# Pair transfers issued by ScalarE instead of GpSimd, and the value read moved ahead of the softmax division on VectorE

## The chip, the cores and the metric

The kernel runs on one core of one Trainium2 chip. The metric is the device time of one launch in microseconds, the median of three runs. Everything is float32: each weight and each activation is split into a high part and a low part, and a product is three matmuls on TensorE.

## The reference

Two transformer blocks for 512 tokens of width 1024. The change lies in the second layer of the first block, the dilated attention:

```python
u = h @ w_in
q, k, v, gate = split(u)                     # 3 groups x 8 heads x 64 each; gate 8 x 64
q = partial_rope(rms_norm(q, q_norm), cos, sin)
k = partial_rope(rms_norm(k, k_norm), cos, sin)
for g, (window, dilation) in enumerate(((128, 1), (512, 4), (2048, 16))):
    o, lse = dilated_band_attention(q[g], k[g], v[g], dilation, window // dilation)
o = softmax-weighted sum of the three o      # weights: softmax over the three lse
x = x + (o * silu(gate)) @ w_out
```

The rotation mixes the first 16 channels of each head: channel d needs channel d + 8, or d - 8. Channels lie on the partitions here, so another partition's values are needed.

## The kernel before

Five engines run programs of their own that meet in semaphores. Each engine takes its own instructions in order. The launch is a list of 15 stages; the change is in stage 4 alone.

**Work of stage 4.** The input projection has 40 weight tiles. They are taken as four chunks (`c` = 0 to 3) of ten steps (`j` = 0 to 9), one tile for each step. A tile is 24 matmuls (8 blocks, three products each) into PSUM bank 0 or 7 in turn. Tiles 0, 1, 3, 4, 5, 6 of a chunk are queries and keys of two heads (`QK_TILES`, `n` counts them from 0 to 23), tiles 2, 7, 8 are values (`V_TILES`), tile 9 is the gate. Chunk c makes the projections of heads 2c and 2c + 1, and beside them the attention of chunk a = c - 1 is computed, in eight units (head half times residue of the position modulo 4). A fifth round (c = 4) has only attention.

**TensorE in step j of chunks 1 to 3**, in this order: the tile (L1599); if j is odd and at least 3, the products of two units with the values (`two_values`, L1823), which need ScalarE's copies of the turned probabilities; the turning of unit j - 1's probabilities, six transposes (`turn_probs`, L1837), which wait for `p_done`; the scores of the next unit (L1794, L1806); in steps 3, 8 and 9 the turning of a value tile (L1887), which for the value tile of step 7 waits until VectorE has done the variance of all six query and key tiles (`var_done`); in steps 1, 2, 4, 5, 6, 7 the sum of squares of the tile before (L1650).

**VectorE in step j**: the variance of tile j - 2 (`head_var`, L995, only if that is a query or key tile; then the tile is finished in this step); maxima of unit j - 1 (L1265 to L1270) and of unit j (L1272); the low part of a coming weight tile (`prep`, L973), which waits for ScalarE's high part; the softmax division of unit j - 1 (reciprocal L1284, multiplication L1285, which gives `p_done`) after ScalarE's exponential; in steps 2, 7, 8 and 9 the read of the value or gate tile j out of PSUM (L1298, L1293), which waits until TensorE has finished tile j; then three instructions of Newton's step (L988 to L990) from ScalarE's guess of 1/sqrt; and the rotation of tile j - 2, four instructions (L1305 to L1308), which gives `n_done`. The rotation reads `at_pair`, where the 16 channels of each head lie with their partners' values. `at_pair` has two buffers, used in turn.

**ScalarE in step j**: the high part of a coming weight tile (`prep`, L457); the copy of the turned probabilities of unit j - 2 (L457, two instructions, `at_PT`); the exponential of unit j - 1 (L717); the guess for 1/sqrt from the variance (`guess_var`, L495 and L496); for a query or key tile the copy out of PSUM into `at_raw` (L457) and the square (L476).

**GpSimd** does nothing in this stage but issue the transfers that fill `at_pair`: four for each query or key tile, 96 in all, each 8 partitions of 512 elements from `at_raw`. For tile n it waits for ScalarE's copy, and for `n_done` of tile n - 2, so that the buffer is free. Tile n - 2 in this counting is: for the tile of step 3, that of step 0 (rotated in step 2); step 4, that of step 1 (rotated in step 3); step 5, that of step 3 (rotated in step 5); step 6, that of step 4 (rotated in step 6); for steps 0 and 1, the ones of the chunk before that were rotated in steps 7 and 8.

Weights are fetched by SyncE, four tiles ahead at most. ScalarE issues some other transfers between its instructions (L638, L667, L690, L691).

Of the kernel before, what the change touches and what calls it, by code (L numbers as in the profile page):

```python
# [66 lines left out]
READ0 = [4 + sum(READS[:n]) for n in range(15)]  # L67
LAST = 14
BARRIERS = ()
PAIR_CLEARED = 3  # L70
PI = 3.1415925
ROUND = 1.5 * 2.0 ** 23
TURN = (6.28125, 0.0019350051879882812, 3.019916e-07)
# [77 lines left out]
def build(nc, weights, x_in, ple_in, pos_in, params_in, consts_in, masks_in, out, spill):  # L151
    ctx = ExitStack()
    with ctx:
# [241 lines left out]
        def slot_bank(j):  # L395
            return 7 * (j % 2)
# [32 lines left out]

        @block.gpsimd  # L430
        def _(pool):
            pool.wait_ge(dve_out, PAIR_CLEARED)
            for c in range(4):
                for i, j in enumerate(QK_TILES):
                    n = len(QK_TILES) * c + i
                    raw = at_raw[:, 6 * (c % 2) + i, :]
                    pool.wait_ge(read_out, READ0[4] + SLOTS * c + j + 1)
                    if n >= 2:
                        pool.wait_ge(n_done, KC + n - 1)
                    for h in range(2):  # L440
                        for to, of in ((0, 8), (8, 0)):
                            pool.dma_start(at_pair[h * HEAD + to:h * HEAD + to + 8, n % 2, :],
                                           raw[h * HEAD + of:h * HEAD + of + 8, :]).then_inc(pair_loaded[n % 2], 16)


        @block.scalar
        def _(act):
# [246 lines left out]
            for c in range(5):  # L694
                a = c - 1
                for j in range(SLOTS):
# [34 lines left out]
                    if c < 4:  # L731
                        k.up(tile_done)
                        k.up(read_out)
                        if j == 9:
                            act.wait_ge(read_out, k.at(read_out))
                            act.activation(at_SG[:, c % 2, :], at_SG[:, c % 2, :], ACT.Silu).then_inc(gated, 1)
                            k.up(gated)
                            logs()
                        elif j in V_TILES:
                            pass  # L740
                        else:
                            act.wait_ge(tile_done, k.at(tile_done))
                            raw = at_raw[:, 6 * (c % 2) + QK_TILES.index(j), :]
                            copy(raw, ps[:, slot_bank(j), :]).then_inc(read_out, 1)
                            act.wait_ge(read_out, k.at(read_out))
                            square(raw)
            split(at_Yh[:, 3, :], 0)
            attention_over(k, unit=(m_done, e_done, t_done, pt_done, o_done), chunk=(n_done,))
            stage_end(act, "act", k, 4)
# [209 lines left out]
        def _(dve):  # L959
# [3 lines left out]
            def link(instr):  # L963

                instr.then_inc(dve_chain, 1)
                dve.wait_ge(dve_chain, k.up(dve_chain))
# [286 lines left out]
            for c in range(5):  # L1253
                a = c - 1
                for j in range(SLOTS):
# [20 lines left out]
                    if c < 4:  # L1276
                        prep()
                        if c == 0 and j == 0:
                            newton(4, 1.0 / D, rx)
                            link(dve.tensor_scalar(ex[:, :], var[:, :], EPS, None, ALU.mult))  # L1280
                    if a >= 0 and 0 <= j - 1 < UNITS:
                        st, probs = at_st[:, u % 4, :], unit_home(a, u)
                        dve.wait_ge(e_done, UNITS * a + u + 1)
                        link(dve.reciprocal(st[:, 3:4], st[:, 2:3]))  # L1284
                        dve.tensor_scalar(probs, probs, st[:, 3:4], None, ALU.mult).then_inc(p_done, 1)  # L1285
                    if c < 4:
                        k.up(tile_done)
                        k.up(read_out)
                        if j == 9 or j in V_TILES:
                            dve.wait_ge(tile_done, k.at(tile_done))  # L1290
                        if j == 9:
                            dve.wait_ge(v_turned, GROUPS * c + 2)
                            dve.tensor_tensor(at_SG[:, c % 2, :], ps[:, slot_bank(j), :], rx[:, :], ALU.mult).then_inc(read_out, 1)  # L1293
                        elif j in V_TILES:
                            g = V_TILES.index(j)
                            if g == 2 or g == 0 and c:
                                dve.wait_ge(v_turned, GROUPS * c + (g == 2))
                            dve.tensor_tensor(value_rows(c, g), ps[:, slot_bank(j), :], rx[:, :], ALU.mult).then_inc(read_out, 1)  # L1298
                    if c < 4 and j - 1 in SUM_SLOT:
                        head_newton()  # L1300
                        n = SUM_SLOT[j - 1]
                        raw, pair = at_raw[:, 6 * (c % 2) + n, :], at_pair[:, n % 2, :]
                        even, odd = ((at_C[:, :], at_S[:, :]), (at_T[:, 0, :], at_T[:, 1, :]))[n % 2]
                        dve.wait_ge(pair_loaded[n % 2], 64 * (3 * c + n // 2 + 1))
                        dve.tensor_tensor(pair, pair, odd, ALU.mult)  # L1305
                        link(dve.tensor_tensor(raw, raw, even, ALU.mult))
                        link(dve.tensor_tensor(raw, raw, pair, ALU.add))
                        dve.tensor_tensor(raw, raw, rs[:, :], ALU.mult).then_inc(n_done, 1)  # L1308
                        dve.wait_ge(n_done, k.up(n_done))
# [996 lines left out]
```

## Time and profile before

| what | value |
|---|---|
| median of three runs | 1955.55 us (1954.84 to 1955.66) |
| time of the profiled execution | 1955.55 us |
| span of its trace | 1953.7 us |
| TensorE busy | 1894.4 us, 97% |
| VectorE, ScalarE, GpSimd busy | 64%, 44%, 3% |
| `at_pair<-at_raw` transfers | 96, 16 KB each, 1.8 us from issue to landing |
| chunk 0, chunks 1 to 3, last round of stage 4 | about 341 to 400, 400 to 654, 654 to 689 us of the span |

The trace is of one execution. Lines such as L1285 are lines of the kernel before. A row of the timeline has the start, the duration, the engine, the line, the operation, what it writes and reads, how many instructions the row merges and, in brackets, how long the engine had been idle before and on whom it waited. An instruction may begin before the recorded end of the one in front of it, since the engines are pipelined.

### The profile page before, as it was taken

The numbers are of one execution on the slowest core, as the hardware profiler recorded it, in microseconds if no ns is written. First come the engines' busy times: TensorE is split into PE (matmuls) and PEld (weight loads), VectorE is DVE, ScalarE is ACT, GpSimd is POOL, SyncE is SP. The second block draws the span as 40 slices with busy tenths as digits, with TensorE's granted clock in tenths as the row PEclk, the third lists the DMA queues.
The fourth block names the chain that finished last, engine by engine and source line by source line (L and its number), as shares of the span: only waits on it lengthen the run. The fifth ranks groups of instructions, "written<-read, shape, count | busy, mean of one in ns | idle before, by whom it ended". The sixth has DMA issues, their size and how long they took to land.

```text
span 1953.7 us, 23354 instructions
## 1 busy us (share of the span) xinstructions
PE 1894.4 (97%) x8436; PEld 1475.2 (76%) x8436; DVE 1250.8 (64%) x1960; ACT 855.2 (44%) x1207; POOL 49.5 (3%) x100
## 2 busy tenths in 40 slices
PE   6999899999999899999999999999999999999999
PEld 4888587777777677888888866666766788888887
DVE  5999888878778668444433375697766654444322
ACT  5443555445445445434332254554354444343321
POOL 0000000211111000000000000000000000000000
PEclk9999999999999899999999999999999999999999
DMA  4333143322222033332333322111221323322333
GB/s 177 97 97 97 59 145 101 110 73 70 67 70 63 30 108 98 97 104 93 100 105 114 128 65 65 54 55 54 76 65 44 112 95 98 106 95 98 97 104 101
DMA packets 51346, 175.32 MB, mean 90 GB/s; under 512 B 7616, under 2 KB 7872, under 8 KB 50624
## 3 DMA queue, kind: packets, MB, share of 16 engines
q1 hardware_dynamic: 44640, 160.19, 25.8%
q10 hardware_dynamic: 3552, 12.44, 1.7%
q0 software_dynamic: 3072, 1.58, 0.4%
q8 instruction: 53, 0.87, 0.2%
q14 instruction: 29, 0.24, 0.0%
HBM read 166.32 MB, written 6.29 MB: 88 GB/s over the span
## 4 chain that ended last, share of the span: by engine, by line
PE 71%; DVE 21%; ACT 5%; issue 3%; DMA 0%; ACTq 0%; DVEq 0%
PE ps L1599 60%; DVE cv_acc L1152 6%; DVE w_lo L973 3%; PE ps L1650 2%; PE ps L1615 1%; PE ps L1794 1%; PE ps L1837 1%; ACT w_hi L457 1%; PE ps L1806 1%; PE ps L1823 1%; DVE ds_acc L1356 1%; PE ps L1992 1%; DVE X L1025 1%; PE ps L2043 1%; DVE ds_mx L1355 1%
## 5 line engine op out<-in xcount | busy, mean ns | idle before, releaser
L973 DVE TENSOR_TENSOR w_lo<-w_raw,w_hi 128x1024 fp32r<-128x1024 f32 x299 | 365.8, 1225 | 339.8 <-ACT w_hi L457 333.7
L1599 PE MATMUL ps<-H_hi,w_hi 128*128 128x512 f32 x1272 | 508.5, 400 | 1.2 <-DVE H_lo L1019 1.2
L1599 PE MATMUL ps<-H_hi,w_lo 128*128 128x512 f32 x1272 | 495.6, 390 | 0.0
L1599 PE MATMUL ps<-H_lo,w_hi 128*128 128x512 f32 x1272 | 495.1, 389 | 0.0
L457 ACT ACTIVATE w_hi<-w_raw 128x1024 fp32r<-128x1024 f32 x299 | 313.0, 1049 | 169.8 <-PE ps L1599 169.1
L1599 PEld LDWEIGHTS ps<-H_hi,w_hi 128*128 128x128 f32 x1272 | 238.8, 188 | 59.5 <-issue 9.3
L1599 PEld LDWEIGHTS ps<-H_lo,w_hi 128*128 128x128 f32 x1272 | 238.9, 188 | 55.3 <-issue 6.7
L1599 PEld LDWEIGHTS ps<-H_hi,w_lo 128*128 128x128 f32 x1272 | 238.7, 188 | 50.8
L1599 PE MATMUL ps<-mid_hi,w_lo 128*128 128x512 f32 x352 | 138.7, 394 | 0.0
L1599 PE MATMUL ps<-mid_hi,w_hi 128*128 128x512 f32 x352 | 138.7, 394 | 0.0
L1599 PE MATMUL ps<-mid_lo,w_hi 128*128 128x512 f32 x352 | 138.7, 394 | 0.0
L1599 PE MATMUL ps<-N_hi,w_hi 128*128 128x512 f32 x280 | 118.4, 423 | 0.7 <-ACT ds_P L835 0.7
L1152 DVE SCALAR_TENSOR_TENSOR cv_acc<-cv_a,par,cv_acc 128x509 f32<-128x509 f32 (+21 forms) x176 | 116.0, 729 | 1.6 <-ACT cv_acc L608 1.6
L457 ACT ACTIVATE mid_hi<-tmp 128x512 f32 x44 | 27.8, 632 | 193.3 <-DVE tmp L1110 193.3
L1599 PE MATMUL ps<-N_hi,w_lo 128*128 128x512 f32 x280 | 112.3, 401 | 0.0
L1599 PE MATMUL ps<-N_lo,w_hi 128*128 128x512 f32 x280 | 112.1, 400 | 0.0
L1599 PEld LDWEIGHTS ps<-mid_hi,w_hi 128*128 128x128 f32 x352 | 65.8, 187 | 16.5
L1599 PEld LDWEIGHTS ps<-mid_hi,w_lo 128*128 128x128 f32 x352 | 65.8, 187 | 16.2
L1599 PEld LDWEIGHTS ps<-mid_lo,w_hi 128*128 128x128 f32 x352 | 65.8, 187 | 16.2
L1106 DVE TENSOR_TENSOR tmp<-ps,rx 128x512 f32<-128x512 f32 x44 | 30.4, 691 | 66.2 <-PE ps L1599 66.2
L1599 PEld LDWEIGHTS ps<-N_hi,w_hi 128*128 128x128 f32 x280 | 53.9, 192 | 22.7 <-issue 9.0
L1599 PEld LDWEIGHTS ps<-N_lo,w_hi 128*128 128x128 f32 x280 | 53.7, 192 | 13.7 <-issue 2.2
(342 smaller groups left out, 2713.0 us busy)
## 6 DMA issues: line engine op xcount, KB each, us to landing
w_raw<-weights SPq DMA_DIRECT2D x299, 512.0 KB, 3.5
X<-x ACTq DMA_DIRECT2D x4, 512.0 KB, 11.4
pl_P<-spill ACTq DMA_DIRECT2D x1, 2048.0 KB, 7.7
spill<-X ACTq DMA_DIRECT2D x8, 256.0 KB, 2.0
X<-spill ACTq DMA_DIRECT2D x2, 1024.0 KB, 5.0
out<-X SPq DMA_DIRECT2D x8, 256.0 KB, 4.6
at_pair<-at_raw POOLq DMA_DIRECT2D x96, 16.0 KB, 1.8
pl_raw<-ple SPq DMA_DIRECT2D x2, 512.0 KB, 12.8
```

What stands on the lines that cost most here:

```text
L457: return act.activation(out_ap, in_ap, ACT.Copy)
L973: dve.tensor_tensor(w_lo[:, s, :], w_raw[:, s, :], w_hi[:, s, :].bitcast(F32), ALU.subtract)\
L1025: dve.scalar_tensor_tensor(X[:, m:m + n, :], src, scale, X[:, m:m + n, :], ALU.mult, ALU.add)\
L1106: dve.tensor_tensor(tmp[:, j, :], ps[:, bank_of(k.n["prep"] - AHEAD - 1), :], rx[:, :], ALU.mult).then_inc(read_out, 1)
L1152: instr = dve.scalar_tensor_tensor(acc, a[:, 0:S - t], w, acc, ALU.mult, ALU.add)
L1355: link(dve.max(ds_mx[:, :], acc))
L1356: link(dve.match_replace(acc, ds_mx[:, :], acc, TAKEN))
L1599: mm = pe.matmul(ps[:, bank, :], w, x, start=first and n == 0 and q == 0, stop=last and n == len(blocks) - 1 and q == 2)
L1615: mm = pe.matmul(ps[:, banks[which], :], w, x[:, b, :], start=b == 0 and q == 0, stop=b == KC - 1 and q == 2, skip_group_check=True)
L1650: pe.matmul(ps[:, bank, :], ones if lhsT is None else lhsT, sq[:, (k.n[sq_done] - 1) % 2, :], start=c == 0, stop=c == n - 1).then_inc(sq_u ...
L1794: mm = pe.matmul(ps[:, near_bank(a, near), :], at_raw[rows, q, r:S:4], at_raw[rows, q + 1, :], start=True, stop=True)
L1806: mm = pe.matmul(ps[:, far_bank(a, far), (g - 1) * P:g * P], at_raw[rows, q + 2 * g, r:S:4], at_raw[rows, q + 2 * g + 1, r:S:4], start=Tru ...
```

## The change

GpSimd's program no longer issues anything. ScalarE issues the four transfers of a query or key tile, right after the square of that tile in its own program, with the same waits in front: the setup of VectorE for the first tile, and `n_done` of tile n - 2 for the others. On VectorE the read of the value tile or the gate tile, with its waits, now stands before the softmax division of unit j - 1 and not behind it.

```diff
         @block.gpsimd
         def _(pool):
-            pool.wait_ge(dve_out, PAIR_CLEARED)
-            for c in range(4):
-                for i, j in enumerate(QK_TILES):
-                    n = len(QK_TILES) * c + i
-                    raw = at_raw[:, 6 * (c % 2) + i, :]
-                    pool.wait_ge(read_out, READ0[4] + SLOTS * c + j + 1)
-                    if n >= 2:
-                        pool.wait_ge(n_done, KC + n - 1)
-                    for h in range(2):
-                        for to, of in ((0, 8), (8, 0)):
-                            pool.dma_start(at_pair[h * HEAD + to:h * HEAD + to + 8, n % 2, :],
-                                           raw[h * HEAD + of:h * HEAD + of + 8, :]).then_inc(pair_loaded[n % 2], 16)
+            k = Counts()
+            for stage in BARRIERS:
+                stage_end(pool, "pool", k, stage)
...
                             act.wait_ge(read_out, k.at(read_out))
+                            n = len(QK_TILES) * c + QK_TILES.index(j)
                             square(raw)
+                            if n == 0:
+                                act.wait_ge(dve_out, k.at(dve_out))
+                            if n >= 2:
+                                act.wait_ge(n_done, normed + n - 1)
+                            for h in range(2):
+                                for to, of in ((0, 8), (8, 0)):
+                                    act.dma_start(at_pair[h * HEAD + to:h * HEAD + to + 8, n % 2, :],
+                                                  raw[h * HEAD + of:h * HEAD + of + 8, :]).then_inc(pair_loaded[n % 2], 16)
...
-                    if a >= 0 and 0 <= j - 1 < UNITS:
-                        st, probs = at_st[:, u % 4, :], unit_home(a, u)
-                        dve.wait_ge(e_done, UNITS * a + u + 1)
-                        link(dve.reciprocal(st[:, 3:4], st[:, 2:3]))
-                        dve.tensor_scalar(probs, probs, st[:, 3:4], None, ALU.mult).then_inc(p_done, 1)
-                    if c < 4:
                         k.up(tile_done)
                         k.up(read_out)
                         if j == 9 or j in V_TILES:
                             dve.wait_ge(tile_done, k.at(tile_done))
...
                             dve.tensor_tensor(value_rows(c, g), ps[:, slot_bank(j), :], rx[:, :], ALU.mult).then_inc(read_out, 1)
+                    if a >= 0 and 0 <= j - 1 < UNITS:
+                        st, probs = at_st[:, u % 4, :], unit_home(a, u)
+                        dve.wait_ge(e_done, UNITS * a + u + 1)
+                        link(dve.reciprocal(st[:, 3:4], st[:, 2:3]))
+                        dve.tensor_scalar(probs, probs, st[:, 3:4], None, ALU.mult).then_inc(p_done, 1)
```

## Rows read from the trace of the kernel before

**Rows 1.** Busy time by stretch, chunk 2: PE, PEld, DVE, ACT, POOL, clock, DMA share, GB/s
```profile
486.00:569.00 83.00, 82.78 (x451) 64.61 (x449) 63.17 (x126) 40.58 (x72) 12.30 (x24) 1.00 0.22 67
```
**Rows 2.** Timeline of TensorE, chunk 2: the transposes of steps 2, 3, 7, 8
```profile
505.26 0.82 PE L1837 MATMUL ps<-con,at_Sm 128*128 128x128 f32 x6
...
515.08 0.87 PE L1837 MATMUL ps<-con,at_Sm 128*128 128x128 f32 x6 [0.22 <-DVE at_Sm L1285]
...
550.84 0.87 PE L1837 MATMUL ps<-con,at_Sm 128*128 128x128 f32 x6
...
559.32 0.82 PE L1837 MATMUL ps<-con,at_Sm 128*128 128x128 f32 x6
```
**Rows 3.** Timeline of VectorE, chunk 2: value reads of steps 2, 7, 8, division of step 3
```profile
505.46 0.69 DVE L1298 TENSOR_TENSOR tmp<-ps,rx 128x512 f32<-128x512 f32 x1 [1.50 <-PE ps L1599]
506.07 0.68 DVE L988 TENSOR_TENSOR rs<-r 128x512 f32<-128x512 f32 x1
...
514.21 0.16 DVE L1284 RECIPROCAL at_st<-at_st 128x1 f32<-128x1 f32 x1
514.40 0.62 DVE L1285 TENSOR_SCALAR at_Sm<-at_Sm,at_st 128x768 f32<-128x768 f32 x1
...
549.92 0.69 DVE L1298 TENSOR_TENSOR at_SG<-ps,rx 128x512 f32<-128x512 f32 x1 [0.93 <-PE ps L1599]
...
559.52 0.69 DVE L1298 TENSOR_TENSOR tmp<-ps,rx 128x512 f32<-128x512 f32 x1 [0.59 <-PE ps L1599]
```
**Rows 4.** Timeline of ScalarE, stage 1: two transfers issued (ACTq) and what follows
```profile
251.84 0.33 ACTq L638 DMA_DIRECT2D spill<-pl_raw  x1
252.21 0.45 ACTq L667 DMA_DIRECT2D rp<-pos  x1
252.71 0.63 ACT L457 ACTIVATE H_hi<-cv_Y 128x512 fp32r<-128x512 f32 x1 [0.90 <-ACT pl_raw L457]
```
**Rows 5.** Line L690 in the view of one tile: duration least/median/most in ns
```profile
L690 ACTq DMA_DIRECT2D at_near<-masks x1: 631/631/631, 338.7 to 338.7; - x1
```
**Rows 6.** Timelines of ScalarE and VectorE, chunk 2, steps 5 to 7
```profile
534.02 0.64 ACT L457 ACTIVATE at_PT<-ps 128x256 f32<-128x256 f32 x2
...
534.59 0.69 DVE L1308 TENSOR_TENSOR at_raw<-at_raw,rs 128x512 f32<-128x512 f32 x1
...
537.66 0.94 ACT L717 ACTIVATE at_Sm<-at_Sm,at_st 128x768 f32<-128x768 f32 x1 [3.01 <-DVE at_st L1270]
...
544.24 0.69 DVE L1308 TENSOR_TENSOR at_raw<-at_raw,rs 128x512 f32<-128x512 f32 x1
...
547.03 1.22 DVE L973 TENSOR_TENSOR w_lo<-w_raw,w_hi 128x1024 fp32r<-128x1024 f32 x1
```
**Rows 7.** Timeline of ScalarE, chunk 0, after the tile of step 4
```profile
367.10 0.63 ACT L476 ACTIVATE sq<-at_raw 128x512 f32<-128x512 f32 x1
367.64 1.04 ACT L457 ACTIVATE w_hi<-w_raw 128x1024 fp32r<-128x1024 f32 x1
368.59 0.62 ACT L495 ACTIVATE r<-var 128x512 f32<-128x512 f32 x1
```
**Rows 8.** Timelines of VectorE and TensorE, chunk 0, steps 5 to 8
```profile
374.16 0.69 DVE L1308 TENSOR_TENSOR at_raw<-at_raw,rs 128x512 f32<-128x512 f32 x1
...
376.94 0.69 DVE L988 TENSOR_TENSOR rs<-r 128x512 f32<-128x512 f32 x1
...
381.17 0.69 DVE L1308 TENSOR_TENSOR at_raw<-at_raw,rs 128x512 f32<-128x512 f32 x1
...
385.49 0.69 DVE L1298 TENSOR_TENSOR at_SG<-ps,rx 128x512 f32<-128x512 f32 x1 [1.64 <-PE ps L1599]
...
391.05 0.69 DVE L995 SCALAR_TENSOR_TENSOR var<-ps,ex 128x512 f32<-128x512 f32 x1
...
391.89 0.72 PE L1887 MATMUL ps<-con,at_SG 128*128 128x128 f32 x4
```
**Rows 9.** Busy time by stretch, in the last round of stage 4
```profile
655.00:660.00 5.00, 2.66 (x12) 1.58 (x9) 3.09 (x10) 1.66 (x3) 0.00 (x0) 0.57 0.00 0
```

More of the change, by code:

```diff
@@ L69 @@
 BARRIERS = ()
-PAIR_CLEARED = 3
 PI = 3.1415925
@@ L745, in _ @@
                             act.wait_ge(read_out, k.at(read_out))
+                            n = len(QK_TILES) * c + QK_TILES.index(j)
                             square(raw)
+                            if n == 0:
[5 more added lines that the diff above has]
+                                    act.dma_start(at_pair[h * HEAD + to:h * HEAD + to + 8, n % 2, :],
+                                                  raw[h * HEAD + of:h * HEAD + of + 8, :])                                        .then_inc(pair_loaded[n % 2], 16)
             split(at_Yh[:, 3, :], 0)
```

## Prediction

> **What bounds the kernel now.** I read the busy time by stretch first, then TensorE's timeline where the change lies, then VectorE's and ScalarE's beside it. In chunk 2 TensorE is busy for 82.78 of 83.00 us at full clock [rows 1]; chunks 1 and 3 look the same. So any time that TensorE has to stand still there is added to the launch, and work on the other engines counts only when TensorE comes to wait for it. Its one wait in each of chunks 1 to 3 is 0.22 us, in step 3, for VectorE's softmax division [rows 2]. The reader should see how close the two engines run: in step 2 the transposes start at 505.26, as the tile ends, and the value read on VectorE starts at 505.46, after VectorE had been idle for 1.50 us, waiting for the tile's last matmul [rows 2, 3]. That idle time shows that the division, which stood before the read, was done long before the tile's end.
>
> **Part one, the reordering.** It acts where a value tile meets a unit: steps 2, 7 and 8 of chunks 1 to 3, nine places. (In step 9 there is no unit, in chunk 0 no attention.) The read must wait for the end of tile j. The division now stands behind it, and TensorE's transposes, which follow the same tile, wait for the division. Two things that were done before the tile ended now come one after the other behind its end.
>
> Step 2: the read starts at 505.46 as before; the next VectorE instruction starts 0.61 later [rows 3], at 506.07: that is now the reciprocal. The multiplication starts 0.19 after it (514.21 to 514.40) and takes 0.62 [rows 3], so it ends at 506.88. TensorE started 0.06 after the end of the multiplication where it waited for it (515.08 against 514.40 + 0.62) [rows 2, 3]. So the transposes start at 506.94 and not at 505.26: 1.68 us. After an interruption the six transposes last 0.87 and not 0.82 [rows 2], which makes 1.73.
>
> Step 3: VectorE's chain from the value read to the next division gets longer by the moved pair, 0.19 + 0.62 = 0.8 us at most, and TensorE has been put back by 1.7, so the 0.22 us wait of step 3 goes. 1.73 - 0.22 = 1.51.
>
> Step 7: an odd step, so two_values fills the time right after the tile. Read 549.92, reciprocal 550.53, multiplication 550.72 to 551.34, transposes 551.40 against 550.84 [rows 2, 3]: 0.56.
>
> Step 8: read 559.52, multiplication's end 559.52 + 0.61 + 0.19 + 0.62 = 560.94, transposes 561.00 against 559.32 [rows 2, 3]: 1.68, with the 0.05 of the interruption 1.73.
>
> A chunk: 1.51 + 0.56 + 1.73 = 3.80; three chunks: 11.4 us. What the reordering could give is an earlier read where VectorE is late. It isn't late: before all three value reads of chunk 2 it had been idle for 0.59 to 1.50 us [rows 3]. The gain is nothing but the 0.22 already counted.
>
> **Part two, the issue on ScalarE.** The 96 issues on GpSimd were hidden, GpSimd has nothing else to do; taking them away gives nothing. On ScalarE they stand in line. The trace shows what an issue costs there: two in a row start 0.37 us apart, the second lasts 0.45, and the next activation, which could have run, starts only at 252.71 after 0.90 us of idle time [rows 4]. Another took 0.63 us [rows 5]. No transfer of 8 partitions is issued by ScalarE in this trace. Its price has nothing as its lower end, since nothing shows that a small one costs what a large one does, and 0.66 (0.63 and a gap) as its upper end. I take 0.37, from the issue whose source is in SBUF as here: 1.48 us for a tile's four. They run beside the square, whose successor started 0.54 after it [rows 7], so ScalarE's next work is 0.94 later.
>
> The Trainium skill, Perfetto Trace Analysis, section on the HWDGE DMA instruction, says that such an instruction holds the sequencer through its semaphore wait, the descriptor generation and any excess semaphore increments, and an activation's wait doesn't. The idle 0.90 agrees for the issue; no row shows a wait in front of one. DMA: Bandwidth & Descriptors, section "Why a DMA increments its semaphore by 16 and not by 1", would have an 8-partition copy use 8 DMA engines, with the other 8 increments written by the sequencer; at the page's some 100 ns for an update an issue would be 0.47, by my estimate, and the total some 2 us more than mine.
>
> The new wait: the transfers of steps 5 and 6 wait for a rotation that ends in the same step. In front of ScalarE's program then stand the next weight part, the turned copy, the exponential and the guess, all of which VectorE needs.
>
> Chunk 2, step 5: the rotation ends at 534.59 + 0.69 = 535.28 [rows 6]. Issues to 536.8, weight part 0.95 (its successor starts that much later in [rows 7]), turned copy 0.64 [rows 6]: the exponential starts at 538.4 and not at 537.66 [rows 6], and the guess and the rotation of step 6 are about 0.7 later. The rotation of step 6 ends at 544.93 + 0.7 = 545.6; issues and ScalarE's weight part make 548.1, VectorE's weight part, 1.22, makes 549.3, and the value read of step 7 is not due before 549.92 [rows 3, 6]. The exponential that the division behind it needs follows 548.1 by the copy's 0.64 and its own 0.94: 549.7, before the division's 550.53. It is hidden. With 0.66 for an issue it isn't: exponential and rotation 1.9 late in step 6, rotation end 546.8, then 2.64 + 0.95 + 1.22 = 551.6, which is 1.7 us after 549.92, in each chunk.
>
> Chunk 0 has shorter steps, and there I find a stall. Its value turning of step 8 starts at 391.89, just after the variance on VectorE (391.05 + 0.69 = 391.74) which it waits for [rows 8]: no slack. After step 4's tile the guess is 0.94 later, and the rotation of step 5 ends at 374.85 + 0.94 = 375.8 [rows 7, 8]. Then issues 1.5, weight part 0.95, guess 1.3 (its two activations) = 3.75, where VectorE before began Newton's step 2.09 after the rotation (376.94 - 374.85) [rows 8]: 1.65 more, together 2.6. The rotation of step 6 ends at 381.86 + 2.6 = 384.5. Issues and weight part to 386.9, VectorE's weight part 1.2 behind, so the value read of step 7 starts at 388.1 and not at 385.49 [rows 8]: 2.6. VectorE has no idle time from there to the variance, so TensorE's value turning is 2.6 late. Chunks 1 to 3 have the division's transposes and a longer step in front, there the same variance is in time.
>
> **Sum.** Profiled execution 1955.55 us (span 1953.7 and 1.85 around it), which is the median as well. 1955.55 + 11.4 + 2.6 = **1969.6 us**, slower by 0.7%.
>
> **Rivals.**
>
> *The issues cost nothing to TensorE* (short ones, or the loop of chunk 0 holds better than I reckon). For it: ScalarE is busy for 40.58 of 83 us [rows 1]. Against it: the 0.90 idle [rows 4]. Time 1955.55 + 11.4 = 1967.0.
>
> *The issues are dear*, 0.66 each. For it: [rows 5]. Chunks 1 to 3 lose 1.7 more each, 5.1; chunk 0's stall goes through three sets of issues, 3 times 1.16 more: 2.6 + 3.5 = 6.1. Time 1955.55 + 11.4 + 5.1 + 6.1 = 1978.2.
>
> *The clock falls.* In the last round TensorE was busy for 2.66 of the 5 us from 655 to 660, and the granted clock of that stretch was 0.57, mostly the lower level, 1.2 GHz [rows 9]. A stall of 2.6 in chunk 0 resembles it, though it comes out of dense work. If it lasts for 12 us of matmuls (my assumption, two or three such stretches), half the clock costs 6: 1975.6.
>
> *Not slower*: the value read ahead pays. VectorE's chain from the read to step 3 sets that step's start, and a read done earlier would free it. Place: step 3 of three chunks; price: the 0.22 of each, 0.7 in all, 1954.9 us. It decides only if the transposes don't wait, that is if the tile's real end lay over 1.7 us before the recorded one. The idle times in front of the reads [rows 3] speak against it.
>
> **How the numbers follow.** Chances: forecast 0.52, issues free 0.16, issues dear 0.14, clock 0.14, not slower 0.04. The forecast's own range is 1966 to 1973. The range of all takes in the two ends of the issue's price and the clock's cost, and allows 3.5 us less for terms of the reordering which other waits may cover: 1963.5 to 1979.5. A measurement of this kernel can tell 0.2%, 3.9 us, from no change. All cases but the last lie above that; leaving something for the reordering being covered: faster 0.02, same 0.03, slower 0.95.
>
> **What would show it.** The transposes on TensorE will wait for the multiplication on VectorE nine times in chunks 1 to 3, 1.3 to 1.7 us in steps 2 and 8 and some 0.5 in step 7, and the wait of step 3 will be gone. VectorE's idle time before the value reads grows by 0.8. The stretch of a chunk lengthens by 3.8. Four ACTq rows stand behind each square, 0.33 us each; in steps 5 and 6 they start with the end of the rotation. TensorE's value turning in step 8 of chunk 0 waits 2.6 us for the variance. What would make it wrong: issues much off 0.37, a wait in steps 4 to 6 that I hold to be covered, or a fall of the clock in a stretch where it is now full.

## The result and the profile after

The changed kernel takes 1983.39 us, the median of 4 runs (1981.53 to 1984.99), against 1955.19 us (1951.89 to 1955.66, 4 runs) for the kernel before. The ratio is 1.0149, with a 95% interval of 1.0134 to 1.0166: slower by 28.2 us. The forecast was 14 us more, and the range ended at 1979.5. The direction was right; the size was half of what it is, and the time lies outside the range. Two executions in the experiments below (one of the kernel before, one of e5_late) took 3128 us at a granted clock of 0.556; the ratios and their intervals leave them out, and the medians move by no more than 0.3 us for them.

The profiled execution took 1984.48 us, with a span of 1982.7 us (before: 1953.7). From the page of the changed kernel, the busy times, and the queue of ScalarE's transfers with packets, MB and share:

```profile
PE 1902.5 (96%) x8436; PEld 1480.5 (75%) x8436; DVE 1251.7 (63%) x1960; ACT 856.0 (43%) x1207; POOL 0.2 (0%) x4
...
q10 hardware_dynamic: 5088, 14.02, 2.1%
```

The work is the same as before, and GpSimd's part of it is gone. Nothing on this page says that ScalarE has become slower, since an issue on ScalarE isn't counted as busy time. It has to be looked at by itself: the view of the tile `at_pair` in the changed kernel, with the least, median and most ns of one issue.

```profile
L746 ACTq DMA_DIRECT2D at_pair<-at_raw x96: 631/632/1242, 344.6 to 659.8; - x96
```

An issue takes 0.63 us and not 0.37. That is the price of the rival "the issues are dear".

**Where in stage 4.** In every kernel here the last score row of a chunk (`ps<-at_raw`, 64x512, in TensorE's timeline) has the same place in the program. From one to the next a chunk takes, in us (chunk 0 from the stage's first row of TensorE, at 341.07 before and 341.20 after; the last round up to the row of L1853 that waits for `at_Yl`, at 688.92 and 719.44):

| kernel | chunk 0 | chunk 1 | chunk 2 | chunk 3 | last round |
|---|---|---|---|---|---|
| before | 57.43 | 84.63 | 84.62 | 84.62 | 36.55 |
| changed | 67.07 | 92.79 | 90.12 | 94.30 | 33.96 |
| difference | +9.64 | +8.16 | +5.50 | +9.68 | -2.59 |

The sum is 30.4 us, and the whole span is 29.0 longer; the 1.5 that come back behind stage 4 were not followed. To be explained are 5.5 us in every chunk with attention, 9.6 in chunk 0, and 2.7 and 4.2 more in chunks 1 and 3, with 2.6 given back in the last round.

**A chunk with attention.** TensorE's timeline in chunk 2 of the changed kernel; [rows 2] have the same transposes before:

```profile
524.85 0.88 PE L1837 MATMUL ps<-con,at_Sm 128*128 128x128 f32 x6 [1.51 <-DVE at_Sm L1298]
...
560.89 0.87 PE L1837 MATMUL ps<-con,at_Sm 128*128 128x128 f32 x6 [0.27 <-DVE at_Sm L1298]
...
570.53 1.09 PE L1823 MATMUL ps<-at_PT,at_V 128*64 128x128 f32 x24 [1.01 <-ACT at_PT L449]
...
572.58 0.87 PE L1837 MATMUL ps<-con,at_Sm 128*128 128x128 f32 x6 [0.95 <-DVE at_Sm L1298]
...
582.72 0.87 PE L1837 MATMUL ps<-con,at_Sm 128*128 128x128 f32 x6 [1.51 <-DVE at_Sm L1298]
```

VectorE beside the first of them, which answers to [rows 3]:

```profile
523.38 0.69 DVE L1293 TENSOR_TENSOR tmp<-ps,rx 128x512 f32<-128x512 f32 x1 [2.22 <-PE ps L1599]
523.98 0.15 DVE L1297 RECIPROCAL at_st<-at_st 128x1 f32<-128x1 f32 x1
524.17 0.62 DVE L1298 TENSOR_SCALAR at_Sm<-at_Sm,at_st 128x768 f32<-128x768 f32 x1
```

This is the order foreseen: read 523.38, reciprocal 0.60 later, multiplication 0.19 later and 0.62 long, transposes 0.06 behind its end. VectorE's idle time before the read went from 1.50 to 2.22 us: it stood ready with the division in hand and waited for the tile. In step 7 the reader sees two waits where 0.56 in all was expected: TensorE waits first for ScalarE's copy of the turned probabilities (1.01) and then for the division (0.95). ScalarE's timeline shows why the copy is late: it stands behind step 6's four issues, and ends at 570.48.

```profile
566.16 2.62 ACTq L746 DMA_DIRECT2D at_pair<-at_raw  x4
568.88 1.06 ACT L449 ACTIVATE w_hi<-w_raw 128x1024 fp32r<-128x1024 f32 x1 [6.56 <-issue]
569.84 0.64 ACT L449 ACTIVATE at_PT<-ps 128x256 f32<-128x256 f32 x2
```

Step 6 has a short wait as well (0.27). The five waits sum to 5.25 us, where before there was one of 0.22.

**Chunk 0.** TensorE's three waits in it, in the changed kernel:

```profile
360.94 0.63 PE L1887 MATMUL ps<-con,tmp 128*128 128x128 f32 x4 [0.57 <-DVE var L996]
...
388.40 1.12 PE L1650 MATMUL ps<-sq,con 128*128 128x512 f32 x2 [2.15 <-DVE var L996]
...
399.06 1.10 PE L1887 MATMUL ps<-con,at_SG 128*128 128x128 f32 x4 [4.05 <-DVE var L996]
```

ScalarE's timeline over steps 4 to 6 of chunk 0, which answers to [rows 7], shows who makes the variance late:

```profile
367.70 2.62 ACTq L746 DMA_DIRECT2D at_pair<-at_raw  x4
370.43 1.06 ACT L449 ACTIVATE w_hi<-w_raw 128x1024 fp32r<-128x1024 f32 x1 [2.09 <-issue]
...
374.24 0.63 ACT L468 ACTIVATE sq<-at_raw 128x512 f32<-128x512 f32 x1
377.68 2.62 ACTq L746 DMA_DIRECT2D at_pair<-at_raw  x4
380.40 1.06 ACT L449 ACTIVATE w_hi<-w_raw 128x1024 fp32r<-128x1024 f32 x1 [5.53 <-PE ps L1599]
...
383.16 0.63 ACT L468 ACTIVATE sq<-at_raw 128x512 f32<-128x512 f32 x1
387.65 2.62 ACTq L746 DMA_DIRECT2D at_pair<-at_raw  x4
390.37 1.06 ACT L449 ACTIVATE w_hi<-w_raw 128x1024 fp32r<-128x1024 f32 x1 [6.57 <-issue]
```

After the square of step 5 (ends 374.87) ScalarE stands for 2.81 us until the rotation is done (377.68), then issues for 2.62, and the next weight part starts after 5.53 us of idle time, where it had started 0.54 after the square of step 4 before [rows 7]. One step later it is 6.57. VectorE shows the consequence: in this row of the changed kernel its low part waits 3.19 us for ScalarE's high part, and variance and value read stand behind it.

```profile
391.53 1.23 DVE L974 TENSOR_TENSOR w_lo<-w_raw,w_hi 128x1024 fp32r<-128x1024 f32 x1 [3.19 <-ACT w_hi L449]
```

Note what the brackets name: "PE ps L1599" and "issue". Neither tells of `n_done`. The wait stands in no row of its own, and the ACTq row begins only when it is over. The Trainium skill, Perfetto Trace Analysis, section on the HWDGE DMA instruction, says that the reported time of such an instruction starts when its semaphores are satisfied. The trace agrees: each of the four-issue rows lasts 2.62 us, whether ScalarE had stood 2.81 us before it or not at all.

**The clock.** Busy time by stretch in the changed kernel, in the order of [rows 1]:

```profile
400.00:404.00 4.00, 4.00 (x11) 3.12 (x11) 3.90 (x7) 2.95 (x4) 0.00 (x0) 0.50 0.40 131
480.00:490.00 10.00, 10.00 (x33) 7.33 (x32) 7.16 (x13) 3.59 (x7) 0.00 (x0) 0.67 0.23 73
664.00:676.00 12.00, 11.22 (x36) 8.04 (x36) 8.00 (x15) 4.47 (x9) 0.00 (x0) 0.72 0.28 87
```

TensorE is busy all of the 4 us from 400, at a granted clock of 0.50, the lower level of 1.2 GHz; in the 10 us from 480, within chunk 1, the clock is 0.67, and in the 12 us from 664, within chunk 3, it is 0.72. In front of the first stood the waits of 2.15 and 4.05 us, and the clock fell before the second of them was over (0.98 from 396 to 398, 0.50 from 398 to 400). The first weight tile behind it took 7.89 us (399.81 to 407.70), where before it took 5.57 (392.37 to 397.94). Finer stretches of chunk 1 show where the second one lies:

```profile
478.00:480.00 2.00, 1.05 (x25) 0.94 (x22) 1.88 (x5) 1.97 (x5) 0.00 (x0) 0.96 0.37 41
480.00:482.00 2.00, 2.00 (x9) 1.67 (x9) 1.91 (x3) 1.38 (x3) 0.00 (x0) 0.50 0.55 221
...
486.00:488.00 2.00, 2.00 (x9) 1.58 (x8) 1.43 (x3) 1.60 (x4) 0.00 (x0) 0.83 0.00 0
488.00:490.00 2.00, 2.00 (x11) 1.65 (x9) 0.00 (x0) 0.58 (x1) 0.00 (x0) 1.00 0.59 139
```

The lower level begins behind the two waits of step 7 (1.01, and 0.95 up to 479.80) and is over before the wait of step 8, which ends at 492.58; in chunk 3 it is the same (0.54 from 664 to 666, 1.00 from 672). So it is no matter of the wait of step 8. Chunk 2 has the same waits and kept the full clock (1.00 from 570 to 584).

The last round goes the other way. Its mean clock was 0.81 before and is 0.90 now:

```profile
652.37:688.92 36.55, 31.08 (x212) 23.00 (x211) 20.36 (x68) 15.82 (x36) 0.00 (x0) 0.81 0.06 19
```
```profile
685.48:719.44 33.96, 28.44 (x211) 21.57 (x210) 20.20 (x68) 15.73 (x36) 0.00 (x0) 0.90 0.05 14
```

### The profile page after: what moved, and what is told of

The parts are those of the page before. It is cut to its first block, busy times and chain, and to the rows that moved or that the text cites. A ratio compares the mean times of both kernels' runs of the same rounds, so it can differ in the third digit from the quotient of the medians.

```text
span 1982.7 us, 23331 instructions
## 1 busy us (share of the span) xinstructions
PE 1902.5 (96%) x8436; PEld 1480.5 (75%) x8436; DVE 1251.7 (63%) x1960; ACT 856.0 (43%) x1207; POOL 0.2 (0%) x4
## 4 chain that ended last, share of the span: by engine, by line
PE 73%; DVE 16%; ACT 5%; issue 3%; ACTq 2%; DMA 0%; DVEq 0%
PE ps L1599 63%; PE ps L1615 2%; DVE w_lo L974 2%; ACTq L746 2%; PE ps L1650 1%; ACT w_hi L449 1%; PE ps L1794 1%; PE ps L1837 1%; DVE cv_acc L1153 1%; DVE ds_acc L1356 1%; PE ps L1992 1%; DVE rs L991 1%; DVE rs L990 1%; DVE X L1026 1%; DVE rs L989 1%
## 5 line engine op out<-in xcount | busy, mean ns | idle before, releaser
L1599 PE MATMUL ps<-H_hi,w_hi 128*128 128x512 f32 x1272 | 511.8, 402 | 1.0 <-DVE H_lo L1020 1.0
L1599 PE MATMUL ps<-H_lo,w_hi 128*128 128x512 f32 x1272 | 497.0, 391 | 0.0
L1599 PE MATMUL ps<-H_hi,w_lo 128*128 128x512 f32 x1272 | 496.9, 391 | 0.0
L1599 PEld LDWEIGHTS ps<-H_hi,w_hi 128*128 128x128 f32 x1272 | 240.3, 189 | 60.9 <-issue 10.1
L1599 PEld LDWEIGHTS ps<-H_lo,w_hi 128*128 128x128 f32 x1272 | 240.1, 189 | 56.4 <-issue 7.5
L1599 PEld LDWEIGHTS ps<-H_hi,w_lo 128*128 128x128 f32 x1272 | 239.9, 189 | 51.0
L1599 PE MATMUL ps<-mid_hi,w_lo 128*128 128x512 f32 x352 | 138.7, 394 | 0.0
L1599 PE MATMUL ps<-mid_hi,w_hi 128*128 128x512 f32 x352 | 138.7, 394 | 0.0
L1599 PE MATMUL ps<-mid_lo,w_hi 128*128 128x512 f32 x352 | 138.7, 394 | 0.0
L1599 PE MATMUL ps<-N_hi,w_hi 128*128 128x512 f32 x280 | 118.4, 423 | 0.7 <-ACT ds_P L836 0.7
L1599 PE MATMUL ps<-N_hi,w_lo 128*128 128x512 f32 x280 | 112.3, 401 | 0.0
L1599 PE MATMUL ps<-N_lo,w_hi 128*128 128x512 f32 x280 | 112.2, 401 | 0.0
L1599 PEld LDWEIGHTS ps<-mid_hi,w_lo 128*128 128x128 f32 x352 | 65.8, 187 | 16.4
L1599 PEld LDWEIGHTS ps<-mid_lo,w_hi 128*128 128x128 f32 x352 | 65.8, 187 | 16.4
L1599 PEld LDWEIGHTS ps<-mid_hi,w_hi 128*128 128x128 f32 x352 | 65.8, 187 | 16.2
L1107 DVE TENSOR_TENSOR tmp<-ps,rx 128x512 f32<-128x512 f32 x44 | 30.4, 690 | 66.3 <-PE ps L1599 66.3
L1599 PEld LDWEIGHTS ps<-N_hi,w_hi 128*128 128x128 f32 x280 | 53.9, 192 | 22.1 <-issue 8.4
L1599 PEld LDWEIGHTS ps<-N_lo,w_hi 128*128 128x128 f32 x280 | 53.8, 192 | 13.7 <-issue 2.2
```

What stands on the lines that cost most here:

```text
L1107: dve.tensor_tensor(tmp[:, j, :], ps[:, bank_of(k.n["prep"] - AHEAD - 1), :], rx[:, :], ALU.mult).then_inc(read_out, 1)
L1599: mm = pe.matmul(ps[:, bank, :], w, x, start=first and n == 0 and q == 0, stop=last and n == len(blocks) - 1 and q == 2)
```

## The experiments

Unless said otherwise each was timed beside the kernel before; "+" is the difference of the medians. An interval that reaches from 0.999 to 1.001 means 2 us either way. All edits are to the kernel before, save that of e11_reorder_late.

### Each part alone

**e1_reorder**: only the hunk of the change that moves VectorE's division behind the value read.

```diff
-                    if a >= 0 and 0 <= j - 1 < UNITS:
-                        ...  # the division
-                    if c < 4:
...
                         if j == 9 or j in V_TILES:
...
+                    if a >= 0 and 0 <= j - 1 < UNITS:
+                        ...  # the same division
                     if c < 4 and j - 1 in SUM_SLOT:
```

> The kernel before with only the reordering on VectorE; GpSimd issues the pair transfers. Theory A (the prediction's sum for the reordering was right, the rest of the loss is the issue on ScalarE): about 11.4 us more than before, ratio 1.0058, nine waits of TensorE's transposes for the division in chunks 1 to 3 (about 1.5, 0.6 and 1.5 us in steps 2, 7, 8), chunk 0 unchanged. Theory B (the reordering itself costs more than reckoned): over 18 us, ratio over 1.009.

Measured: 1965.24 us (before 1954.18), ratio 1.0054 [1.0041, 1.0067], +11.1. TensorE's waits from 340 to 690 us (waiting line, releaser; us in total, times, longest), and three sets of transposes of chunk 2:

```profile
PE ps L1836 <- DVE at_Sm L1297: 10.5, 9, 1.5
```
```profile
511.80 0.87 PE L1836 MATMUL ps<-con,at_Sm 128*128 128x128 f32 x6 [1.51 <-DVE at_Sm L1297]
...
521.38 0.88 PE L1836 MATMUL ps<-con,at_Sm 128*128 128x128 f32 x6
...
557.50 0.88 PE L1836 MATMUL ps<-con,at_Sm 128*128 128x128 f32 x6 [0.49 <-DVE at_Sm L1297]
```

Nine waits in chunks 1 to 3, 1.51 in steps 2 and 8 and 0.49 in step 7; the wait of step 3 is gone (521.38). A chunk is 88.1 us long, 3.5 more than before, and chunk 0 is as before (57.45). The first part of the prediction holds.

**e2_issue**: only the other part; GpSimd's loop goes, ScalarE issues behind the square.

```diff
+                            n = len(QK_TILES) * c + QK_TILES.index(j)
                             square(raw)
+                            if n == 0:
+                                act.wait_ge(dve_out, k.at(dve_out))
+                            if n >= 2:
+                                act.wait_ge(n_done, normed + n - 1)
+                            for h in range(2):
+                                for to, of in ((0, 8), (8, 0)):
+                                    act.dma_start(at_pair[...], raw[...]).then_inc(pair_loaded[n % 2], 16)
```

> The kernel before with only the issue of the pair transfers on ScalarE; the division stays ahead of the value read. Theory A (an issue takes 0.63 us, four stand in front of ScalarE's next weight part, and in steps 5 and 6 they start only with the end of the rotation): chunk 0 about 6 us longer, chunks 1 to 3 about 2 us longer each in step 7 because the exponential comes late, falls of the clock on top: 12 to 18 us, ratio 1.006 to 1.009. Theory B: hidden but for a few us, ratio under 1.003.

Measured: 1971.88 us (before 1954.18), ratio 1.0090 [1.0077, 1.0103], +17.7. Chunk 0 is 9.7 us longer (67.13), and each later chunk 2.6 (87.2). Its waits from 340 to 690 us:

```profile
PE ps L1888 <- DVE var L996: 4.6, 2, 4.0
PE ps L1838 <- DVE at_Sm L1286: 3.5, 9, 0.7
PE ps L1824 <- ACT at_PT L449: 3.0, 3, 1.0
PE ps L1651 <- DVE var L996: 2.1, 1, 2.1
```

The rows of 3.0 and 3.5 us are those of chunks 1 to 3: in each of them 1.00 and 0.67 in step 7, 0.27 in step 8, and the 0.22 of step 3 as before. So the greater part of the loss is from the issues, and the step "it is hidden" for chunks 1 to 3 falls. The two parts sum to 28.8, the change costs 28.2.

### What of the issue costs: the wait, the length, or both

**e3_wait**: GpSimd issues as before; ScalarE only waits, where the changed kernel does.

```diff
+                            n = len(QK_TILES) * c + QK_TILES.index(j)
                             square(raw)
+                            if n >= 2:
+                                act.wait_ge(n_done, normed + n - 1)
```

> The kernel before, GpSimd issues the transfers as before, but ScalarE waits after each square for the same rotation as in the changed kernel. Theory A (the wait alone is covered, it hurts only with four long issues behind it): within 0.2% of before, no new wait of TensorE. Theory B (the wait is the cost, the issues are not): more than 5 us slower, TensorE's stall in step 8 of chunk 0 there.

Measured: 1954.47 us (before 1954.18), ratio 0.9999 [0.9990, 1.0008]: nothing. The wait is there, in ScalarE's timeline of chunk 2, step 5:

```profile
532.38 0.63 ACT L476 ACTIVATE sq<-at_raw 128x512 f32<-128x512 f32 x1
535.16 1.06 ACT L457 ACTIVATE w_hi<-w_raw 128x1024 fp32r<-128x1024 f32 x1 [2.15 <-DVE at_raw L1311]
```

ScalarE stands 2.15 us for the rotation, and the covers that the prediction counted are enough for that. Here, with no issue between, the releaser is named rightly.

**e5_late**: the issues, with their wait, one step later on ScalarE, behind the guess of the next step; VectorE as before.

```diff
+            def pairs():
+                ...  # the waits and the four transfers of the tile in pending
                     if c < 4 and j - 1 in SUM_SLOT:
                         k.up(sq_used)
                         guess_var()
+                    pairs()
...
+                            n = len(QK_TILES) * c + QK_TILES.index(j)
                             square(raw)
+                            pending.append((n, raw))
```

> The issue on ScalarE, but one step later: the four transfers of a tile stand behind the guess of the next step, where ScalarE has been idle for 1.6 us or more; the division stays ahead of the value read. By then the buffer is long free. Theory A (place and wait make the cost, not the engine): at most 3 us slower than before. Theory B (2.6 us of issue on ScalarE cost their time wherever they stand): 8 us slower or more.

Measured: 1955.46 us (before 1954.18), ratio 1.0002 [0.9993, 1.0010]: nothing, or 2 us at most. ScalarE's timeline in chunk 2:

```profile
529.35 2.62 ACTq L696 DMA_DIRECT2D at_pair<-at_raw  x4
532.01 0.60 ACT L449 ACTIVATE at_raw<-ps 128x512 f32<-128x512 f32 x1 [2.04 <-PE ps L1608]
```

All 96 issues with the full 2.62 us for four, but they end by 531.97, and ScalarE would have waited for the tile up to 532.01 anyway. An issue of 0.63 is no cost in itself; its place is.

**e7_sync**: SyncE issues them between its weight fetches.

```diff
+            for t in range(4 * 14, 4 * 25):
+                ...  # the fetch of weight tile t
+                step = t - TILES0[4] - 7
+                if 0 <= step < 4 * SLOTS and step % SLOTS in QK_TILES:
+                    ...  # the waits and the four transfers of the tile of this step
```

> The kernel before, with SyncE issuing the pair transfers between its weight fetches, same waits. Theory A (what matters is whether the issuing engine has anything behind the issues that others need soon; SyncE's fetches run steps ahead): within 0.2% of before. Theory B (fetches queued behind the waits come late): TensorE waits for weights, over 4 us slower.

Measured: 1955.37 us, ratio 1.0003 [0.9993, 1.0012]: nothing. The same price shows there (view of `at_pair`):

```profile
L435 SPq DMA_DIRECT2D at_pair<-at_raw x96: 624/625/792, 345.7 to 631.5; - x96
```

So 0.63 goes with the transfer and not with ScalarE, and SyncE, four tiles ahead with its fetches, can bear it.

**e6_two16**: ScalarE issues behind the square, but two transfers of 16 partitions and not four of 8. The partners are then not swapped, so the rotation of this kernel reads other values than the reference's.

```diff
+                            ...  # the waits of the changed kernel
+                            for h in range(2):
+                                act.dma_start(at_pair[h * HEAD:h * HEAD + 16, n % 2, :],
+                                              raw[h * HEAD:h * HEAD + 16, :]).then_inc(pair_loaded[n % 2], 32)
```

> As the run with only the issue on ScalarE, but two transfers of 16 partitions for each tile in place of four of 8; they copy the channels without the swap, so the rotation gets wrong partners and only the time counts. Theory A (an issue costs 0.63 us whatever its partitions, so the number of issues sets the price): 1.3 us for a tile, near the 1.48 of the prediction's sum, which gave 2.6 us in chunk 0 and nothing in chunks 1 to 3: 1 to 4 us over before. Theory B (the 0.63 come from having only 8 partitions): 0.33 us each, 0.7 us for a tile, under 1 us over before.

Measured: 1957.92 us (before 1954.33), ratio 1.0019 [1.0009, 1.0029], +3.6. An issue takes 0.53 and the two 1.17 us, 1.45 less than four of the changed kernel. Its `at_pair` row and its one wait on the variance:

```profile
L745 ACTq DMA_DIRECT2D at_pair<-at_raw x48: 527/530/1082, 344.5 to 634.4; - x48
```
```profile
PE ps L1887 <- DVE var L995: 2.3, 1, 2.3
```

There is one wait, in chunk 0, and no loss in chunks 1 to 3 (84.6 each); chunk 0 is 3.8 us longer (61.27). Besides the wait that is clock: it was granted at 0.77 in the 4 us from 396, behind the wait. The place is the one that the prediction named, and the size is near its 2.6, but that was worked out for 1.48 us a tile. Its own steps with 1.17 give 387.1 for the value read of step 7, where they had given 388.1 for 1.48 and 385.49 stands for the kernel before: 1.7 us, and 2.3 were measured. So the working of chunk 0 was short by some 0.7 even where the issues are short.

### Which of the issues

Three kernels share the issues between ScalarE and GpSimd, each with semaphores of its own; `by_act` says which tiles are ScalarE's. VectorE has its order of before.

```diff
+def by_act(c, j):
+    return j not in (5, 6)   # e8_no56;  e9_chunk0: c == 0;  e10_only56: j in (5, 6)
```

**e8_no56**: ScalarE has the tiles of steps 0, 1, 3 and 4, whose wait is over early; GpSimd those of steps 5 and 6.

> ScalarE issues the transfers of the tiles of steps 0, 1, 3 and 4, whose buffer is free by then; GpSimd issues those of steps 5 and 6, which wait for a rotation of their own step. Division ahead of the value read. Theory A (the loss needs the late wait and the long issues together): at most 2 us over before. Theory B (16 sets of 2.6 us in ScalarE's way are enough): two thirds of the 17.7 us of all 24 sets, over 8 us.

Measured: 1957.09 us (before 1954.33), +2.8 by the medians; the ratio, 1.0009 [0.9999, 1.0018], says 1.8, and up to 3.5 by its end. In the trace chunk 0 is 0.9 us longer (58.36), with waits of 0.57 in step 3 and 0.35 in step 8, and the others are as before (84.63).

**e9_chunk0**: ScalarE issues in chunk 0 alone.

> ScalarE issues the transfers of chunk 0 (six tiles), GpSimd those of chunks 1 to 3; the division ahead of the value read. Theory A (chunk 0 with its short steps takes over half of the issue's loss: two waits of TensorE for the variance, 2.1 and 4.0 us, and a fall of the clock behind them): chunk 0 about 9.6 us longer, chunks 1 to 3 as before, 8 to 11 us in all. Theory B (each tile's issue costs alike): a quarter of 17.7, 4.4 us.

Measured: 1963.08 us (before 1954.34), ratio 1.0047 [1.0030, 1.0064], +8.7. Chunk 0 is 9.6 us longer (67.01), the others are as before (84.64). Its waits, and the stretch behind the last of them:

```profile
PE ps L1909 <- DVE var L1014: 4.6, 2, 4.1
...
PE ps L1672 <- DVE var L1014: 2.1, 1, 2.1
```
```profile
400.00:404.00 4.00, 4.00 (x10) 3.04 (x10) 3.86 (x7) 2.75 (x4) 0.00 (x0) 0.50 0.41 131
```

6.8 us of waits (0.5, 2.1 and 4.1) and the clock at 0.50 behind them make up chunk 0's 9.6.

**e10_only56**: ScalarE has steps 5 and 6 alone.

> ScalarE issues only the transfers of the tiles of steps 5 and 6 in each chunk, the ones that wait for a rotation of their own step; GpSimd the other sixteen. Theory A (wait and long issue together make the loss, the other sets only add to chunk 0): chunks 1 to 3 about 2.6 us longer each as with all sets, chunk 0 some 2 us less than with all: 13 to 17 us. Theory B (a third of the sets, a third of the loss): 6 us.

Measured: 1968.79 us (before 1954.34), ratio 1.0074 [1.0057, 1.0091], +14.4, with the 87.2 us for a chunk of e2_issue, and chunk 0 longer by 6.6 (64.04). So the third of the issues whose wait ends late makes 14.4 of the 17.7 us, and the other two thirds without these some 2 (e8_no56).

**e11_reorder_late**: the changed kernel with the late place of e5_late.

> The changed kernel, but ScalarE issues the transfers of a tile one step later, behind the guess. Theory A (the two parts add up and the late issue costs nothing): the reordering's 11.1 us alone, ratio 1.0054, each of chunks 1 to 3 longer by 3.5 us. Theory B (the parts act on each other through ScalarE's delay of the exponential): over 14 us.

Measured: 1965.71 us (before 1954.34), ratio 1.0058 [1.0041, 1.0075], +11.4: what the reordering costs alone (11.1). Of the change's 28.2 us the place of the issues makes 16.8.

### The price of an issue

**p1_probe**: the kernel before, with 27 more transfers on ScalarE at the very end, of several shapes; it ran once, and its time says nothing. `con` and `rs` are in SBUF, `spill` is in DRAM.

```diff
+            probes = [...]        # (to, of) in groups of one shape
+            for group in probes:
+                for to, of in group:
+                    act.dma_start(to, of).then_inc(probed, 16)
+                    sent += 1
+                act.wait_ge(probed, 16 * sent)
```

> The kernel before with 28 transfers more, issued by ScalarE at the very end of its program, where nothing depends on them: 8, 16 and 32 partitions, four in a row each, then 8 short rows, 8 rows out of DRAM, 64 and 128 partitions, within SBUF and out of DRAM. The duration of each ACTq row is the price of an issue. Theory A (SBUF to SBUF is what makes an issue 0.63 us): all of SBUF to SBUF at 0.63, those out of DRAM at 0.33. Theory B (few partitions make it): 8 partitions at 0.63 from either place, 128 at 0.33. Theory C (each issue costs 0.63 when another has just been issued): the first of four shorter than the next three.

Measured, one row for each shape: 8 partitions within SBUF; 16 partitions within SBUF; 8 partitions out of DRAM; 128 partitions within SBUF; 128 out of DRAM.

```profile
1946.95 0.63 ACTq L969 DMA_DIRECT2D rs<-con  x1
...
1950.83 0.61 ACTq L969 DMA_DIRECT2D rs<-con  x1
...
1961.11 0.32 ACTq L969 DMA_DIRECT2D rs<-spill  x1
...
1970.81 0.48 ACTq L969 DMA_DIRECT2D rs<-con  x1
...
1975.32 0.35 ACTq L969 DMA_DIRECT2D rs<-spill  x1
```

Within SBUF an issue took 0.48 to 0.67 us in all shapes (the very first of all 1.27), out of `spill` 0.28 to 0.35, of 8 partitions as of 128. A quarter of the bytes with 8 partitions (512 bytes a row in place of 2048) changed nothing (0.63 to 0.67). So in the probe the price hangs on the two ends. It isn't the whole rule: of the kernel's own loads out of DRAM on ScalarE, `rp<-pos` takes 0.45 [rows 4], `at_near<-masks` 0.63 [rows 5] and `at_far<-masks` 0.63 too, and no run here says why.

The prediction's estimate from the Trainium skill, DMA: Bandwidth & Descriptors, section "Why a DMA increments its semaphore by 16 and not by 1", added 0.1 us to an issue for the increments that the sequencer writes where a copy uses fewer than 16 DMA engines. The 0.1 was an estimate from the page's figure for a semaphore update after the receipt; the page has none for these writes. The traces don't bear such increments out as the main cause of the 0.63: 8 partitions out of DRAM cost 0.32, less than 128 do (0.35), and within SBUF 8 and 16 partitions differ by 0.02 in the probe. The 0.53 of e6_two16 against 0.63 can't settle whether some of it is theirs, since its transfers add 32 to the semaphore and not 16.

## Why the prediction was wrong in size

**What bounds the kernel, and what the reordering does: right.** 11.4 us were forecast, 11.1 measured in e1_reorder, with the nine waits at their places and their lengths (1.51 and 0.49 of waiting), the wait of step 3 gone and the idle time before the read longer. By the trace it is 3.5 for a chunk and not 3.8. The rival on the other side, that the early read pays, fell.

**The step that failed is a term of the sum: "I take 0.37, from the issue whose source is in SBUF as here".** It measured 0.63, 0.66 from one to the next, 2.62 us for a tile's four and not 1.48. The row that it was taken from, `spill<-pl_raw` [rows 4], goes to DRAM; the probe shows transfers out of `spill` at half the price of those within SBUF. The likeness in the source alone was the wrong likeness. The upper bound, 0.66, was the right price, that of the rival "the issues are dear". That it was within the bounds is in part luck: its row [rows 5], `at_near<-masks`, is a load out of DRAM.

**From that term followed two others.** In chunk 0 the forecast was 2.6 and the dear rival's 6.1; the waits are 6.8 (0.57 in step 3, 2.15 in step 7, 4.05 in step 8). The chain was the one described, but it showed in three places where I had looked at one: step 3's value turning waits for the variance too, and so do the sums of squares of step 7, behind the late rotation of step 6. The issues of the steps before step 4 were left out of the chain, and e10_only56, which has neither them nor step 4's, has no wait in step 3 and one of 0.77 and not 2.15 in step 7; e6_two16 shows the working short by 0.7 with short issues as well. In chunks 1 to 3 the forecast was nothing and the dear rival's 1.7 each; the issues alone cost 2.6 (e2_issue), and 2.0 on top of the reordering (5.50 of chunk 2 less 3.5). The place was step 7, as foreseen; but I followed only the value read and the division there. TensorE waits first for ScalarE's turned copy (1.01 us of it), which stands behind the same issues; that wait is a step that was missing, not a size. In the forecast's own numbers the copy ends at 548.7, before the 549.81 at which TensorE took it; at 0.66 an issue it ends at 551.0, 1.2 late. TensorE's row in the kernel before:

```profile
549.81 1.10 PE L1823 MATMUL ps<-at_PT,at_V 128*64 128x128 f32 x24
```

**The mechanism by which it costs was right, and needs both its halves.** The wait in front of ScalarE's program alone costs nothing (e3_wait), nor do long issues where ScalarE would be idle (e5_late), and they cost little where their wait is over (e8_no56, 0.9 in the trace, 1.8 by the ratio). Wait and issues together cost 3.6 where the issues are short (e6_two16) and 17.7 where they are long (e2_issue), 14.4 of it by the two tiles of a chunk whose wait ends late (e10_only56).

**The clock was a rival, and came on top of the dear case.** Chunk 0's 9.6 are 6.8 of waits and 2.8 to 2.9 more, with the clock at 0.50 behind the last wait. Chunks 1 and 3 have 2.7 and 4.2 more than chunk 2, with stretches at 0.67 and 0.72. In e1_reorder and in e2_issue all of the chunks 1 to 3 are alike (88.1 and 87.2); step 7 of e2_issue has waits of 1.00 and 0.67 where the changed kernel has 1.01 and 0.95. The last round, which before has its own stretch at 0.57 [rows 9], gives 2.6 back with its mean clock at 0.90 in place of 0.81. I had made clock and price alternatives of each other, with one chance each, though the larger waits of the one brought the other with them; hence the range ended too low.

The sum again, by the trace: reordering 3 times 3.5 = 10.5; issues in chunk 0 9.6, clock and all; in chunks 1 to 3 6.0; clock in chunks 1 and 3 less the last round's 2.6: 2.7 + 4.2 - 2.6 = 4.3. Together 30.4, the table's sum. Against the forecast's 14.0 that is 7.0 more in chunk 0, 6.0 in the chunks after it, 4.3 of clock, and 0.9 less for the reordering.

**What stays open.** Why chunks 1 and 3 lost the clock and chunk 2, with the same waits, did not: no run tells that apart. The lower level begins right behind step 7's two waits both times, and with 0.67 in place of the second of them (e2_issue) it never came; that these two waits bring it about is argued from this, not shown, and the trace is of one execution. A third buffer of `at_pair`, which would take the wait itself away while the issues keep their place, wasn't tried. No version found beats the kernel before: the best ones (e3_wait, e5_late, e7_sync) equal it.

## What to carry to other kernels

Before an issue is moved to a computing engine, take its price from a row with the same two ends (0.63 within SBUF was not the 0.33 of SBUF to DRAM) or from a probe, count all that a tile needs, and ask what stands behind it in that engine's program when its wait ends last; the same transfers cost nothing measurable one step later in the same program (e5_late). A read placed ahead of ready work, in front of a wait that ends late, puts that work behind the wait: where the engine shows idle time before the read, as here (0.59 to 1.50 us), an earlier place gains nothing. Where two causes of stalls fall in the same steps, reckon them and the clock together and not as alternatives.

## What the hardware showed that I had not expected

Issuing a transfer on ScalarE or SyncE took 0.63 us with both ends in SBUF for 8 partitions, 0.53 (e6_two16) to 0.61 (probe) for 16 and still 0.48 for 128, but 0.28 to 0.35 out of `spill` in DRAM, though other loads out of DRAM took 0.45 and 0.63; GpSimd's issues of the same transfers last 0.52 by its trace (518 ns before). Four small ones in a row thus hold ScalarE 2.62 us, about as long as VectorE's rotation of a tile takes (four instructions of 0.69). And a stall of 4 us in dense matmuls was followed by 4 us and more with the clock at 0.50, in three kernels in the same place (the changed one, e2_issue, e9_chunk0), so that 6.8 us of waiting cost 9.6; in e10_only56, with waits of 0.8 and 4.1 there, chunk 0 lost 6.6 for 4.8.
